# Reordering three stages of a gated attention decoder: paired stick-breaking steps, interleaved memory projections, four score banks

## The reference, cut to what matters

```python
# stick-breaking, for each block of 128 queries
log_keep = jax.nn.log_sigmoid(-z)
r_local = lax.cumsum(log_keep, axis=4, reverse=True)
r_later = lax.cumsum(totals, axis=3, reverse=True) - totals
a = jnp.exp(z + r_local + r_later[..., None])
outs.append(jnp.einsum('bhqk,bkhd->bqhd', a.astype(v.dtype), vb))
...
# memory keys and values
mkv = jnp.einsum('bmd,de->bme', rms_norm(mem, mem_ln_g), w_mem_kv)
km, vm = jnp.split(mkv, 2, axis=-1)
```

## Time and profile before

| what | value |
|---|---|
| median of 3 runs | 1390.65 us (1389.37 to 1392.71) |
| profiled execution, device time | 1388.89 us |
| its span | 1387.1 us |
| PE busy | 1329.0 us, 96% |
| DVE, ACT, POOL busy | 498.7, 667.5, 693.8 us (36%, 48%, 50%) |
| mean granted TensorE clock | 0.985 of full speed |

### The profile page before, as it was taken

How to read it: one execution, slowest core, us unless ns; L and a number is a source line. 1 busy time by engine, 2 the same in 40 slices (tenths; PEclk the granted TensorE clock), 3 DMA queues, 4 the chain that set the end, 5 groups by cost and what they waited for, 6 DMA issues and landing times. The chain is left out here.

```text
span 1387.1 us, 17627 instructions
## 1 busy us (share of the span) xinstructions
PE 1329.0 (96%) x6234; PEld 1037.4 (75%) x6234; DVE 498.7 (36%) x765; ACT 667.5 (48%) x1233; POOL 693.8 (50%) x571
## 2 busy tenths in 40 slices
PE   7999899988999999999999998999889999999998
PEld 6778778865677788887877786886556768888876
DVE  4675332343341222223338724114442412222221
ACT  5554423566354644554445542247644445455431
POOL 3676522354242467767447753224432425776662
PEclk9999999999999999999999999999999999999999
DMA  7553311121222243444355522112122213344432
GB/s 222 159 131 102 87 39 39 39 54 39 61 59 56 48 123 101 110 108 114 101 163 146 130 84 69 39 31 54 46 49 50 69 46 88 102 108 113 107 114 84
DMA packets 210031, 120.78 MB, mean 87 GB/s; under 512 B 9752, under 2 KB 200472, under 8 KB 209944
## 3 DMA queue, kind: packets, MB, share of 16 engines
q1 hardware_dynamic: 209944, 119.66, 32.9%
HBM read 107.04 MB, written 6.29 MB: 82 GB/s over the span
## 5 line engine op out<-in xcount | busy, mean ns | idle before, releaser
L1633 POOL TENSOR_TENSOR w_lo<-w_raw,w_hi 128x512 fp32r<-128x512 f32 (+1 forms) x404 | 501.5, 1246 | 623.5 <-ACT w_hi L1165 574.6
L747 PE MATMUL dense<-h_hi,w_hi 128*128 128x512 f32 x1168 | 502.8, 430 | 2.2 <-DVE h_lo L1346 2.1
L747 PE MATMUL dense<-h_hi,w_lo 128*128 128x512 f32 x1168 | 460.1, 394 | 0.0
L747 PE MATMUL dense<-h_lo,w_hi 128*128 128x512 f32 x1168 | 459.8, 394 | 0.0
L747 PEld LDWEIGHTS dense<-h_hi,w_hi 128*128 128x128 f32 x1168 | 222.4, 190 | 69.6 <-issue 21.9
L1165 ACT ACTIVATE w_hi<-w_raw 128x512 fp32r<-128x512 f32 (+1 forms) x401 | 232.7, 585 | 62.8 <-PE dense L747 62.6
L747 PEld LDWEIGHTS dense<-h_lo,w_hi 128*128 128x128 f32 x1168 | 222.3, 190 | 53.8 <-issue 14.4
L747 PEld LDWEIGHTS dense<-h_hi,w_lo 128*128 128x128 f32 x1168 | 221.3, 189 | 48.6
L1439 DVE TENSOR_TENSOR sig<-dense,x_rstd_row 128x512 f32<-128x512 f32 x48 | 33.2, 692 | 208.0 <-issue 122.8
L1441 DVE TENSOR_TENSOR raw<-dense,x_rstd_row 128x512 f32<-128x512 f32 x80 | 55.1, 688 | 122.4 <-PE dense L747 98.9
L1218 ACT ACTIVATE sig<-sig 128x512 f32<-128x512 f32 x48 | 30.3, 632 | 123.1 <-DVE sig L1439 123.1
(11 more groups left out here) (261 smaller groups left out, 1916.4 us busy)
## 6 DMA issues: line engine op xcount, KB each, us to landing
w_raw<-in_w_in SPq DMA_DIRECT2D x292, 256.0 KB, 2.9
w_raw<-in_w_out SPq DMA_DIRECT2D x32, 256.0 KB, 2.8
x_scratch<-v_dil SPq DMA_DIRECT2D x16, 256.0 KB, 3.4
w_raw<-in_w_mem_kv SPq DMA_DIRECT2D x16, 256.0 KB, 2.7
v_dil<-x_scratch SPq DMA_DIRECT2D x16, 256.0 KB, 2.8
turned<-normed SPq DMA_DIRECT2D x48, 64.0 KB, 2.4
inv_den<-o_norm SPq DMA_DIRECT2D x48, 64.0 KB, 2.4
silu_z<-in_mem SPq DMA_DIRECT2D x4, 512.0 KB
```

Of the source, the lines that this page charges most:

```text
L747: return nc.tensor.matmul(o, lhsT, rhs, start=start, stop=stop, skip_group_check=True)
L1633: pool.tensor_tensor(w_lo[:, g % SPLIT_SLOTS, c], w_raw[:, g % RAW_SLOTS, c], f(w_hi[:, g % SPLIT_SLOTS, c]), ALU.subtract).then_inc(w_lo_ ...
```

## The change

In `plan_layer` the stick-breaking steps are issued by pairs of heads. For pair step s: both `sb_z`, both `sb_soft`, both `sb_pv` of two pair steps before, both `sb_sum` of the one before, both `sb_plus`. The memory steps move up into the group of dilated queries and keys, and the four memory tiles stand between the first four dilated value tiles. The ring of `probs` slots for the memory tokens shrinks from three to one, since the other two hold cosine products in that group. Chunks 1 and 3 of the dilated row scores go to the banks `O` and `A0`.

```diff
-            order = [(p, j, e) for p in range(2) for j in reversed(range(TT)) for e in range(2)]
-            for s in range(len(order) + 4):
-                for kind, lag in (("sb_z", 0), ("sb_sum", 3), ("sb_pv", 4), ("sb_plus", 1), ("sb_soft", 0)):
+            order = [(p, j) for p in range(2) for j in reversed(range(TT))]
+            for s in range(len(order) + 2):
+                for kind, lag in (("sb_z", 0), ("sb_soft", 0), ("sb_pv", 2), ("sb_sum", 1), ("sb_plus", 0)):
                     if 0 <= s - lag < len(order):
-                        yield (kind, *order[s - lag])
-                if s >= 4 and order[s - 4][1:] == (0, 1):
-                    yield ("pair", b, order[s - 4][0])
+                        for e in range(2):
+                            yield (kind, *order[s - lag], e)
+                        if kind == "sb_pv" and order[s - lag][1] == 0:
+                            yield ("pair", b, order[s - lag][0])
...
-    dense([new(kind, DIL, i) for kind in "qk" for i in range(6)], [("room",), ("x_sum",)] + [("room",)] * 14, lag=2)
-    dense([new("v", DIL, i) for i in range(6)] + pair_of("z", DIL),
-          [("room",)] * 5 + [("mem_square",), ("mem_scale",)] + [("mem_t", c) for c in range(4)], lag=2)
-    dense(pair_of("mk", MM) + pair_of("mv", MM), lag=2)
-
+    dense([new(kind, DIL, i) for kind in "qk" for i in range(6)], [("room",), ("x_sum",)] + [("room",)] * 6
+          + [("mem_square",), ("mem_scale",)] + [("mem_t", c) for c in range(4)] + [("room",)] * 2, lag=2)
+    dense([new(*t) for v, t in enumerate((("mk", MM, 0), ("mk", MM, 1), ("mv", MM, 0), ("mv", MM, 1)))
+           for t in (("v", DIL, v), t)] + [new("v", DIL, i) for i in (4, 5)] + pair_of("z", DIL), lag=2)
...
-        mem_ring = Ring(P_SLOTS, [(c, mem_lo_ready, c) for c in range(4)])
+        mem_ring = Ring(1, [(c, mem_lo_ready, c) for c in range(4)])
...
+        def in_out_bank(s):
+
+            return s[0] == "row" and s[1] == DIL and s[3] % 2 == 1
+
...
-                score_users.append((s, row_max, s[1:]))
+                (out_users[s[2] % 2] if in_out_bank(s) else score_users).append((s, row_max, s[1:]))
...
+        def score_bank(s):
+            return (O, A0)[s[2] % 2] if in_out_bank(s) else R[score_ring.slot(s)]
+
+        def score_free(s):
+            return (out_ring[s[2] % 2] if in_out_bank(s) else score_ring).before(s)
```

More of the change, by code:

```diff
@@ L900, in _ @@
                         for s_ in heads:
-                            wait(pe, score_ring.before(s_))
-                        both = [(s_[2], rows_of(s_[2]), R[score_ring.slot(s_)]) for s_ in heads]
+                            wait(pe, score_free(s_))
+                        both = [(s_[2], rows_of(s_[2]), score_bank(s_)) for s_ in heads]
                         banded = rconst[:, M_CAUSAL - 2:M_BAND - 1:M_BAND - M_CAUSAL, :]
@@ L1537, in _ @@
                         dve.wait_ge(*row_done.of(key))
-                        src = R[score_ring.slot(s)]
+                        src = score_bank(s)
                         def negated(out_, in_):
```

## The result

The changed kernel takes 1364.12 us (median of 4 runs, 1362.3 to 1367.68) against 1390.01 (4 runs) of the kernel before: a ratio of 0.9827, interval 0.9807 to 0.9847, so 25.9 us faster. The forecast was 1378 with a range from 1366 to 1388. The profiled execution took 1364.64 us (span 1362.9, 24.2 less than before). PE is busy 1319.6 us and its mean clock is 0.988.

The account below looks back on a forecast made before the run. PE was taken as the bound, with only its gaps and clock able to give time back. Terms +3 - 4.8 - 9.3 - 1.5 = -12.6 us took the profiled 1388.9 to 1376.3, median 1378, range 1366 to 1388.

Parts of the forecast that it names:

- Part 1: Memory projections: 6.9 us of gaps removed, 9.7 us of new stalls added, +3 us; bounds -6.9 and +6.7.
- that loop gets no shorter when it is late: DVE's round among dilated queries and keys, evictions every 6.14 us, was taken as unable to shorten when DVE lags.
- stalls on evictions: From the fourth key tile to the third value tile, PE waits for late DVE evictions: 4.8 us a layer.
- signs of error: A PE wait at the memory turns, waits for low halves of weights, or stick-breaking gaps above 8 us a layer.
- hidden after all: Rival: the moved memory work causes no new stalls, so the memory projections give -6.9 and the time is 1368 us; chance 0.25.
- Part 2: Dilated row scores: two chunks in flight remove most of 5.8 us of waits for maxima, -4.8 us; bounds -5.8 and 0.
- the 0.5 us a layer that I left for DVE's evictions: Dilated row scores: remaining wait expected because DVE is also held by evictions, 0.5 us a layer.
- Part 3: Stick-breaking: the new step order leaves 6.0 us of waits a layer, gaining 9.3 us; bounds -17.6 and -3.
- the forget turn: Stick-breaking: DVE meets a copy not yet made directly ahead of the forget-gate chain; 1.1 us a layer left.
- the last product: End of stick-breaking: this wait stays because the same steps stand around it as before, at 2.2 us a layer.
- ACT standing for the scan: Last stick-breaking pair: ACT's resulting queue leaves waits of 1.4 us at the value product and 0.6 at the sum.
- Clock: Stages with gaps lose 8.6 us to slow clock; fewer gaps give back -1.5 us; bounds -8.6 and +4.

Follow-up runs that it names:

- dve_filled: Kernel before plus two extra DVE bank copies ahead of the eviction of each dilated query and key tile; 1389.29 us, ratio 1.0008.
- memory_late: Changed kernel with the memory tiles behind dilated value tiles 2 to 5 instead of 0 to 3; 1356.66 us, ratio 0.9777.
- forget_last: Changed kernel with the forget tile moved behind the keys of the forgetting branch; 1373.6 us, ratio 0.9898.
- busy_waits: Kernel before plus 29 zero-product matmuls a layer ahead of seven stick-breaking waits; 1382.91 us against 1390.49, ratio 0.995.
- a_only: Kernel before with the memory edit and its ring alone; 1387.52 us against 1388.74, ratio 0.9988.
- late_banks: memory_late with odd chunks of the memory and forgetting branches' row scores also in the output banks; 1353.74 us, ratio 0.974.

## Why the prediction was wrong, point by point

**Part 1, +3 us; measured -1.7 (0 to -3).** The step that failed is "that loop gets no shorter when it is late". dve_filled showed the loop taking 1.42 us more work for 0.3 us, and the changed kernel has a round of 5.46 us behind the scaling. So none of the 9.7 us of stalls on evictions came. The gaps of 6.9 us at the memory tiles went as predicted. In their place came waits that the sum had at nothing: those for low halves (5.1 us against 1.3), because items have a lead of three, which wasn't enough among short tiles, and 1.1 us at the first memory turns. Both had been named as signs of error. The rival "hidden after all" was right on DVE and wrong on the time, since the chain of weights took most of it back; memory_late gets it.

**Part 2, -4.8 us; measured -8 (-6 to -10).** Mechanism right. All 5.8 us of idle time went, and the 0.5 us a layer that I left for DVE's evictions doesn't exist. The rest is an estimate of what a wait costs beyond its idle time, and in layer 0 a share of clock (0.93 to 0.95). In layer 1, at 0.95 in both traces, the stage fell by 3.57 and its idle time by 3.98 - 1.10 = 2.88, which leaves 0.69 us for some five waits, 0.14 each. A clock given to two digits leaves some 0.5 us open in that figure.

**Part 3, -9.3 us; measured -18 (-16 to -21) alone, 16.7 in the two traces.** The step list walked was right: I left 6.0 us of idle time a layer, and there are 5.5 and 6.6; the idle time fell by 9.3, the number forecast. That it agrees to a tenth is luck, since the single waits were off by up to 0.9 us either way. Of them, the forget turn (1.1) has 1.3 to 1.4, the value product (1.4) 1.5, the sum (0.6) 1.3, the last product (2.2) 1.3 and 2.3. The cause that I gave for the last pair, ACT standing for the scan, fell with forget_last. What failed is that a wait was priced at its idle time alone. By busy_waits the old order without slow places takes 78.0 us and the new one 71.7, 12.6 in both layers; 9.3 of this is idle time. The remaining 3.3 fall to some thirteen waits fewer, 0.25 each. That is an upper estimate, since in the trace of before the slow places had used up some of the idle time.

**Clock, -1.5 us; about -4.1 in stick-breaking alone.** This term was mis-sized, though the bound of -8.6 covered it. The slow places cost 4.6 us there before, and the one that is left costs 0.5; with the 12.6 us above that makes the 16.7 of part 3. Layer 0's dilated rows and columns have a share besides.

By the profiled pair the sum reads: part 1 +0.8, dilated attention -8.7, stick-breaking -16.7, and the start of the kernel +0.5, together -24.1 of 24.2. (The 2.0 us of idle time that the memory edit takes from the first row maxima, by a_only, is counted under dilated attention here.) The forecast of -12.6 was half of that. Most of the miss is price per wait (restart and clock, 7.4 us in part 3 and 2.9 in part 2) and the sign of part 1. Both go the same way, so the time fell below the range. One pair of traces carries this sum; single executions of one kernel differ by several us (the changed one 1362.3 to 1367.7).

**What stays open.** The dilated column scores have slow clock in every kernel of the study, in windows in which PE counts as busy throughout (before: 215 to 220 us, PE busy 5.00, clock 0.66). Their count changes from kernel to kernel without an edit there, and nothing here tells why. Nor is it settled what the restart of 0.14 to 0.25 us consists of, nor the part of memory_late's gain beyond its idle time, nor why the first row-maximum wait goes with the memory edit.

## What to carry to other kernels

When waits of the busiest engine are removed, price each at its idle time, some 0.2 us more (here an estimate of 0.14 to 0.25), and a share of the slow clock that follows clusters of waits; here that doubled the gain. Where a wait can't be removed, filling it with zero products into a bank that TensorE owns gives back the clock part without a change of the order. And before a duration is used as the price of an operation, look at its minimum too: 0.69 against a median of 1.65 us meant a collision in time, not work, and 1.42 us of extra work a round on that engine was free.

## What the hardware did that I had not expected

- **More matmuls, less time.** 58 zero products made the kernel 7 us faster (0.995, 0.9934 to 0.9967). At a granted clock of 0.50 (1.2 GHz) dense matmuls of late_banks start 0.42 us apart, and at 1.00 (2.4 GHz) 0.23:

```profile
320.79 0.63 PE L757 MATMUL dense<-h_lo,w_hi 128*128 128x512 f32 x1
321.21 0.63 PE L757 MATMUL dense<-h_hi,w_lo 128*128 128x512 f32 x1
...
322.24 0.40 PE L757 MATMUL dense<-h_hi,w_hi 128*128 128x512 f32 x1
322.47 0.39 PE L757 MATMUL dense<-h_lo,w_hi 128*128 128x512 f32 x1
```

- **VectorE and GpSimd hold each other.** Coinciding, VectorE's addition took 1.65 us and GpSimd's product 1.72; apart, 0.69 and 1.29. 1.42 us of added work moved them apart and lengthened the round by 0.3.
